# The gate products of a solve slot: four pieces of four weight tiles at every other place, in place of eight pieces of two

## The reference

```python
h = rms_norm(x, mix_norm[layer])
p = h @ w_in_first                       # layer 1: w_in_rest
gate_a = p[..., :D_MODEL]
gate_b = p[..., D_MODEL:GATE_WIDTH]
...
y_a = chunked_sgu(...)
y_b, v_first = rwkv7_time_mix(...)       # a recurrence over the tokens, 16 heads of 64
merged = (jax.nn.sigmoid(gate_a) * (y_a @ w_proj_a[layer])
          + jax.nn.sigmoid(gate_b) * (y_b @ w_proj_b[layer]))
```

## Time and profile before

| | |
|---|---|
| median of 3 runs | 2818.41 us (2817.64 to 2821.33) |
| profiled execution | 2810.02 us, span 2808.3 us, granted clock 0.991 |
| PE busy | 2723.9 us, 97% of the span |
| PEld busy | 2600.6 us, 93% |
| DVE busy | 2128.6 us, 76% |
| ACT busy | 1565.8 us, 56% |
| chain that ended last | PE 76%, DVE 13%, ACT 5%, DMA 4% |
| slots with gate products | about 364 to 540 us and 1156 to 1333 us of the span |

### The profile page before, as it was taken

How to read it: one execution, slowest core, us unless ns; L and a number is a source line. 1 busy time by engine, 2 the same in 40 slices (tenths; PEclk the granted TensorE clock), 3 DMA queues, 4 the chain that set the end, 5 groups by cost and what they waited for, 6 DMA issues and landing times.

```text
span 2808.3 us, 61154 instructions
## 1 busy us (share of the span) xinstructions
PE 2723.9 (97%) x26372; PEld 2600.6 (93%) x26372; DVE 2128.6 (76%) x3179; ACT 1565.8 (56%) x2377; POOL 13.9 (0%) x23
## 2 busy tenths in 40 slices
PE   7999999999999999999999999899999989999999
PEld 7999878899999998888999999888999989998899
DVE  7878667678888777666788798667888876777875
ACT  6545644456555455544465555476656646766663
POOL 0000000000000000000000000000000000000000
PEclk9999999999999999999999999899999999999999
DMA  6675311246766753211456667533775774342454
GB/s 233 247 295 181 135 40 43 89 165 233 263 221 246 284 202 130 76 47 47 166 210 247 234 237 264 195 121 121 255 277 207 260 257 155 147 150 106 152 196 149
DMA packets 72941, 511.12 MB, mean 182 GB/s; under 512 B 8480, under 2 KB 9248, under 8 KB 11872
## 3 DMA queue, kind: packets, MB, share of 16 engines
q1 hardware_dynamic: 72672, 507.22, 49.7%
HBM read 506.13 MB, written 1.05 MB: 181 GB/s over the span
## 4 chain that ended last, share of the span: by engine, by line
PE 76%; DVE 13%; ACT 5%; DMA 4%; issue 2%; SPq 0%; DVEq 0%; ACTq 0%
PE solve_banks L2056 11%; PE solve_banks L2058 11%; PE solve_banks L2057 11%; DVE split_halves L1358 4%; PE linear_banks L2050 4%; PE linear_banks L2051 3%; PE linear_banks L2052 3%; PE linear_banks L2056 3%; PE linear_banks L2057 3%; PE linear_banks L2058 3%; DMA raw_units<-in_stream 3%; PE linear_banks L2623 3%; PE linear_banks L2624 3%; PE linear_banks L2625 3%; PE solve_banks L2485 1%
## 5 line engine op out<-in xcount | busy, mean ns | idle before, releaser
L1358 DVE TENSOR_TENSOR split_halves<-raw_units,split_halves 128x1024 fp32r<-128x1024 f32 x806 | 972.3, 1222 | 313.8 <-ACT split_halves L944 311.3
L944 ACT ACTIVATE split_halves<-raw_units 128x1024 fp32r<-128x1024 f32 x806 | 839.5, 1054 | 441.0 <-DMA raw_units<-in_stream 204.2
L2056 PE MATMUL solve_banks<-h_split,split_halves 128*128 128x256 f32 x1792 | 497.9, 278 | 3.8 <-DVE split_halves L1358 3.6
L2058 PE MATMUL solve_banks<-h_split,split_halves 128*128 128x256 f32 x1792 | 497.2, 277 | 0.0
L2057 PE MATMUL solve_banks<-h_split,split_halves 128*128 128x256 f32 x1792 | 497.2, 277 | 0.0
L2056 PE MATMUL solve_banks<-hidden_split,split_halves 128*128 128x256 f32 x1408 | 391.5, 278 | 0.0
L2058 PE MATMUL solve_banks<-hidden_split,split_halves 128*128 128x256 f32 x1408 | 391.1, 278 | 0.0
L2057 PE MATMUL solve_banks<-hidden_split,split_halves 128*128 128x256 f32 x1408 | 391.1, 278 | 0.0
L2056 PEld LDWEIGHTS solve_banks<-h_split,split_halves 128*128 128x128 f32 x1792 | 337.4, 188 | 5.2 <-DVE split_halves L1358 2.5
L2058 PEld LDWEIGHTS solve_banks<-h_split,split_halves 128*128 128x128 f32 x1792 | 337.4, 188 | 0.0
L2057 PEld LDWEIGHTS solve_banks<-h_split,split_halves 128*128 128x128 f32 x1792 | 336.5, 188 | 0.0
(11 more groups left out here) (341 smaller groups left out, 5862.8 us busy)
## 6 DMA issues: line engine op xcount, KB each, us to landing
raw_units<-in_stream SPq DMA_DIRECT2D x403, 1024.0 KB, 4.9
raw_units<-in_mod_w SPq DMA_DIRECT2D x72, 1024.0 KB, 6.0
x<-in_x SPq DMA_DIRECT2D x4, 256.0 KB, 5.5
w2a<-in_w2a SPq DMA_DIRECT2D x2, 512.0 KB, 6.1
w_rows<-in_w SPq DMA_DIRECT2D x2, 512.0 KB, 7.6
bs_rows<-in_bs SPq DMA_DIRECT2D x2, 512.0 KB, 8.2
spatial_t<-in_ws_t SPq DMA_DIRECT2D x2, 512.0 KB, 10.3
out<-x SPq DMA_DIRECT2D x4, 256.0 KB, 4.2
```

Source lines behind the costliest of these rows:

```text
L944: nc.scalar.activation(split[:, n % SPLIT_SLOTS, 0, :], raw[:, item % RAW_SLOTS, (n % 2) * HALF * P:(n % 2 + 1) * HALF * P], ACT.Copy).the ...
L1358: V.tensor_tensor(split[:, n % SPLIT_SLOTS, 1, :], raw[:, item % RAW_SLOTS, (n % 2) * HALF * P:(n % 2 + 1) * HALF * P], split[:, n % SPLIT ...
L2056: M(bank[:, 0:T], w_hi, a[:, 0, :], start=start, stop=False, skip_group_check=True)
L2058: return M(bank[:, 0:T], w_lo, a[:, 0, :], start=False, stop=stop, skip_group_check=True)
```

## The change

The gate pieces are issued at places 3, 5, 7 and 9 alone, behind z0, z1, z2 and z3, and each has four tiles (12 matmuls). Those behind p0, p1, p2 and p3 are gone. The number of the piece is now its index in the list of places. The slot's gate bank counts as filled at place 9, in place of place 10.

```diff
-GATE_STEPS = range(3, 11)
+GATE_STEPS = range(3, 11, 2)
 GATE_TAKEN = 10
 SPLIT_STEPS = (4, 7)
...
             def part_products(key, w, acts, i, steps):
 
-                n = i - steps[0]
+                n = steps.index(i)
                 first, last = TPU * n // len(steps), TPU * (n + 1) // len(steps)
```

## The result

| | before | changed |
|---|---|---|
| median | 2817.64 us (5 runs, 2813.96 to 2821.33) | 2828.69 us (5 runs, 2823.38 to 2833.08) |
| ratio | 1 | 1.0049, 95% interval 1.0032 to 1.0067 |
| profiled execution, span | 2808.3 us | 2821.7 us |
| solve stretch of layer 0, from z0 of slot -1 to the last z4 (place 0 of slot 7) | 176.5 us (363.46 to 539.99) | 182.8 us (357.33 to 540.16) |
| the same of layer 1 | 176.5 us | 182.8 us |

The changed kernel is slower: the medians differ by 11.0 us, 0.4%, and the ratio of the runs, 1.0049, has an interval that reaches from 9 to 19 us. Both solve stretches together are 12.6 us longer.

The account below looks back on a forecast made before the run. PE was taken to set the solve's pace, with DVE's merge just about hidden by work between p and z. Slot terms summed to 6.1 us per layer, 12.2 for two, added to 2818.4: 2830.6 us, range 2823 to 2838.

Parts of the forecast that it names:

- z0 to z1: Time between these stages in a slot: +0.69 us in c = -1, +0.12 in 0, 1, 3, 5, +0.35 in 2, 4, 6.
- z1 to z2: Time between these stages: +0.06 us in slots 0 and 1, -0.14 in 2, 4, 6, -0.33 in 3 and 5.
- z2 to z3: Time between these stages: DVE sets it before and after the change, -0.04 us each in slots 0 to 6.
- z3 to z4: Time between these stages: +0.69 us in every slot, 3.05 to 3.74 in the pattern slot, six matmuls now ahead of p3.
- the transposes: First transpose after z4 in c = 2 and 4: gate bank fills earlier, so 0.20 us comes back each.
- The answer of 1.56 us: From p's start through DVE's merge to the next z: no z can start earlier than 1.56 us after its p.
- 0.86 is what 5.62 leaves for that product: In z1 to z2 of c = 2, 4, 6, the variance product between p1 and rhs1 was put at 0.86 us.
- How soon a stage follows p: Second-half stage directly behind p: 0.12 us taken, 0.22 as upper bound, the 0.10 more carried as 2 us in all.
- Faster: Rival: joining pieces removes 64 entries of 0.105 us and the transposes get 0.8 back, giving 2811 us; chance 5%.
- No difference: Rival: DVE's chain sets the time at most places, so PE's order would not matter and time stays 2818 us; 8%.
- Clock: Rival: short new waits lower TensorE's clock from 2.4 to 1.2 GHz, adding 88 us, so 2918 us; chance 3%.
- Entries: Skill's rule on entering gate pieces: entry costs nothing, so a double piece takes 1.61 us, not 1.50; sum 7 us higher.

## Why the prediction was right

*Time.* Forecast 2830.6, range 2823 to 2838, measured 2828.7; against its own kernel before +12.2 forecast, +11.0 measured. That the medians agree within 2 us is luck: the interval of the difference reaches from 9 to 19 us, and the runs of each kernel spread over 7 to 10 us. The stretches are the test of the mechanism. The sum for them, 6.1 us a layer, measured 6.3, and a part of that is luck too, since the errors of the terms cancel: z0 to z1 +2.22 forecast and +1.96 measured, z1 to z2 -0.96 and -0.51, z2 to z3 -0.28 and -0.19, z3 to z4 +5.52 and +5.37, the transposes -0.40 and -0.33.

*The answer of 1.56 us.* Right to 0.02: p3 to z4 reads 1.54 with nothing between (1.63 in slot 6). The kernels with a shorter merge show that it is DVE's and not PE's.

*z3 to z4, +0.69 in 16 slots.* Measured +0.66 to +0.68 in all 16, 85% of the sum; moving that piece alone gave 5.0 of the 6.3.

*z0 to z1.* Forecast +0.69 in slot -1 (+0.66), +0.12 where p0 had waited for ACT (+0.08 to +0.13), +0.35 in c = 2, 4, 6 (+0.29 to +0.33). The last was read a little too high: z0's first record in slot 2 stands at 429.39, 0.11 before the group of 15 in the earlier trace rows and not 0.05, so the distance was 3.88 before and not 3.81.

*z1 to z2.* Slots 0 and 1 +0.06 (+0.07, +0.03), slots 3 and 5 -0.33 (-0.28, -0.30). Slots 2, 4 and 6 are the mis-sized term: forecast -0.14, measured -0.01, -0.03 and 0.00. The step that failed is "0.86 is what 5.62 leaves for that product". In the changed kernel, rhs1 starts 0.96 after the variance product (434.25 to 435.21):

```profile
433.63 0.27 PE L2494 MATMUL solve_banks<-z,inverse_blocks 64*64 64x64 f32 x1
...
434.25 1.13 PE L2418 MATMUL linear_banks<-k,constants 128*128 128x512 f32 x2
435.21 0.55 PE L2522 MATMUL solve_banks<-v,scores 128*128 128x64 f32 x4
...
435.97 0.44 PE L2485 MATMUL solve_banks<-inverse_blocks,scores 64*64 64x64 f32 x7
```

The 0.86 was a remainder of a sum in which the gate piece behind the product had been charged its full 0.81. Before, product and piece took 1.68 together:

```profile
436.44 1.12 PE L2418 MATMUL linear_banks<-k,constants 128*128 128x512 f32 x2
...
438.12 0.56 PE L2522 MATMUL solve_banks<-v,scores 128*128 128x64 f32 x4
```

So the piece was worth only 0.72 there, and taking it away won that much less. Six such places make 0.7 us.

*z2 to z3.* Forecast -0.04 for c = 0 to 6; measured -0.03 to -0.04 in slots 0, 1, 3, 5 and 6, 0.00 in 2 and 4. The bound is as the prediction had it: in slots 0 to 6 DVE's merge starts 3.43 to 3.44 after z2 in the kernel before, in the changed one, and with the pieces behind p, an altogether different order on PE. What failed is "DVE sets it in both orders". Before the change the merge for z3 was this:

```profile
418.42 0.72 DVE L1866 COPY_PREDICATED inverse_blocks<-level_masks,solve_banks 128x512 f32<-128x512 int8 x1
```

It ended at 419.14, and z3 came 0.10 later and not 0.06: PE's own work set z3, and DVE's answer would have allowed it 0.04 earlier. In the changed kernel the same distance is 0.06, DVE's, in slots 0, 1, 3, 5 and 6, and 0.09 in slots 2 and 4, where PE's order still sets it.

*The transposes.* A return of 0.20 was forecast for c = 2 and 4; 0.17 and 0.16 were measured.

*How soon a stage follows p.* I carried 0.10 more as an upper bound and summed with the lower. The upper is right; the 0.10 lies between the stage's first product and its second. rhs1 of slot 1 on PE, before and then changed:

```profile
414.23 0.55 PE L2522 MATMUL solve_banks<-v,scores 128*128 128x64 f32 x4
414.62 0.44 PE L2524 MATMUL solve_banks<-state,alpha_rho 128*128 128x128 f32 x2
```

```profile
410.22 0.66 PE L2522 MATMUL solve_banks<-v,scores 128*128 128x64 f32 x4
410.72 0.44 PE L2524 MATMUL solve_banks<-state,alpha_rho 128*128 128x128 f32 x2
```

Its second product comes 0.50 after its first in place of 0.39. It cost nothing there, since DVE's answer was still open, as the prediction had it for u0 and rhs1. At y of slots 2 and 4 it did cost: y takes 1.01 in place of 0.91 there, PE sets z3, and z2 to z3 stays at 4.25.

*The rivals.* Faster: the joining did win PE time, 2.3 us of busy time a stretch (3.4 us forecast), and it was spent on waiting. No difference: z1 to z2 and z2 to z3 of slot -1 did not move at all, 3.82 and 4.01; there, four distances in both layers, DVE set the time whatever PE's order was, as the forecast had it too. Clock: the granted clock is 1.00 in both stretches with 13 us of short idle times in each, and it did not fall. What the Trainium skill tells of short idle times between groups of matmuls ("TensorE: Matmul & The Clock Gate", "A second HAM failure mode: psum-queue depth-cycling") did not happen here. Entries: twelve matmuls took 1.47 until the next stage (402.87 to 404.34), less than two pieces of six, 1.61. What the prediction made of the other section of the Trainium skill's page, that joining would win nothing ("Step-by-step: what each phase is for"), does not agree with this.

## What to carry to other kernels

Where two engines hand a chain to and fro, each hand-over has an answer time: from the start of the products to the start of what needs their result. Here it was 1.54 us through DVE wherever DVE had nothing else to do first, and longer where it had (1.83 at z3 of slot -1). Filler work belongs where that time stands open: the same six matmuls cost 0.04 us or less behind p3 and their whole 0.68 us ahead of it. So add up, for each gap, the answer and what the engine has of other work in it; pieces of equal size need not fit the gaps.

And read the difference from the distances in the stretch that changed: those of the two layers agree within 0.03 us, where the runs of the whole program spread over 7 to 29 us and did not tell 0.2%.

## What the runs showed of the hardware that I had not expected

Stretches of the program that are the same in all these kernels differ between executions by more than the change did. From the end of the second solve to the end of the program, in the kernel before and in the two with the shorter merge, the changed one first (one profiled execution each; the last two on the same chip):

```profile
1332.82:2808.30 1475.48, 1429.24 (x12400) 1395.42 (x12400) 1128.35 (x1602) 864.08 (x1306) 0.00 (x0) 0.99 0.54 195
```

```profile
1334.07:2809.30 1475.23, 1429.36 (x12400) 1395.98 (x12400) 1128.22 (x1602) 864.70 (x1305) 0.00 (x0) 0.99 0.53 195
```

```profile
1329.01:2823.90 1494.89, 1450.66 (x12401) 1417.11 (x12400) 1131.81 (x1602) 869.03 (x1306) 0.00 (x0) 0.99 0.52 193
```

The third takes 19.4 us more than the first and 19.7 more than the second for the same instructions, at the same granted clock to two digits. It is not idle time: PE is busy for 21.4 us longer. From the start of one 256-column matmul to that of the next (counted in the trace, neighbours on PE alone) there are 0.105 to 0.113 us in 5873 cases and 0.114 to 0.120 in 4675 in the first, 5776 and 4766 in the second, 2728 and 7813 in the third. In the changed kernel's own execution, where this part takes 1485.1 us, it is 4093 and 6462. Each trace is of another kernel, so that it is the execution and not the kernel is only made likely, by the spread of 28 us in 35 runs of the kernel before. What makes a long stretch of the same matmuls run at the one or the other pace stays open; no run here was made to tell. The solve stretches, whose lengths agree within 0.1 us between the layers of a trace in all but one kernel (0.15), do not show it.
